# Value products of a two-layer attention issued behind a step's transposes in place of in front of them

## The chip, the cores and the metric

The kernel runs on one core of one Trainium2 chip. The metric is the device time of one execution in microseconds (us); less is better. All data are float32; most products are made of three matmuls over a high and a low part of each operand.

## The reference

The program computes two pairs of transformer layers, one after the other, on 512 tokens of width 1024 (batch 1). The first pair is a mixer with window attention, Fourier mixing and a short convolution, and is not touched here. The second pair (`hybrid_layer`, run for two layers) is, per layer and cut to what matters:

```
a_in, b_in, c_in = split(x @ w_in)
o_a = dilated_mixture(...)        # 6 heads of 64, bias and band as one mask
o_b = rms_norm(diff_attention(...)) # 4 heads: (softmax(q1 k1) - lam * softmax(q2 k2)) @ v
o_c = causal_attention(...)       # 6 heads, q and k of 96, v of 64
h = layer_norm(ALPHA * x + concat(o_a, o_b, o_c) @ w_o)
x = layer_norm(ALPHA * h + (silu(h @ w_gate) * (h @ w_up)) @ w_down)
```

All three attentions are causal, so a block of 128 queries number i (0 to 3) needs 128 (i + 1) keys.

## The kernel before

The program is written out engine by engine, with semaphores between them. The weights come as tiles of 128 x 2048 through three buffers; ScalarE writes each tile's high part, GpSimd its low part (L927). The change lies in the attention sweep of the second pair's layers.

**Units.** A unit is one head and one block of queries. A head of kind b has two maps, so each of its blocks gives two units, called first and second here; heads of kinds c and a give one. There are 80 units (`UNITS`, L705), and 64 of them are turned and multiplied with the values (`RANKS`): a first map is not, it is folded into its second. The first eight units are scored earlier, among the projections.

**Steps.** TensorE, VectorE and ScalarE go through the same steps, 5 to 83. For unit s, in step s:

- TensorE scores it (`score`, L2252 for kinds b and c, L2248 and L2249 for a) into one of three banks.
- VectorE adds the mask and takes the minimum (`scored`, L2986), out of PSUM into one of five buffers `sc`. The rows are negated, so that this is the maximum.
- ScalarE takes the exponential in place (`exp2`, L1563 for kind b, L1566 else).
- Two steps later, if the unit is a second map, VectorE joins the two maps (`pair`, L2994, L2995 and L2996): second times a ratio plus first. The result is what the transposes of a second map read.
- Four steps later TensorE turns it (L2367): i + 1 transposes of 128 x 128 into one of three other banks. They wait for `s_paired` (a second map) or `s_probs` (any other), and for the bank.
- ScalarE copies the turned rows to SBUF (L1602, into places called `raw`, `pt_rows`, `pt_cos` and `pt_vc` by the trace).

**Groups.** The turned units are gathered in 13 groups (`GROUPS`) of 4 to 6 units: four blocks of one head of kind c or a, and the b units that fall among them. `mix(g)` issues the products of a whole group with the values (L2346), 20 to 32 matmuls of 64 or 65 columns (two records of the trace each) into one of two banks; it waits for ScalarE's copy of every unit. It is issued in the step that turns the second unit behind the group's last. VectorE takes the rows of a group out (`rows_out2`, L3050 to L3062) one turned unit later. Group 12, the last, is issued among the first matmuls of the output projection (L2384).

The twelve steps and what they turn (kind, head and block of queries; a second map has a double prime):

```
group   0    1      2    3    4      5    6      7    8    9    10   11
turned  c0.3 b1.2"  c2.3 c3.0 b2.2"  c5.0 b3.0"  a1.3 a2.0 a3.0 a4.0 a5.2
```

Every few steps TensorE also turns a finished 128-column chunk of the attention's output (`turn_chunk`, L2325); ScalarE writes its high part (L1616), VectorE its low part (L2530). Its bank is one of the two of the groups.

Of the kernel before, what the change touches and what calls it, by code (L numbers as in the profile page):

```python
# [262 lines left out]
def _program(nc, I, out, seen):  # L263
    ctx = ExitStack()
    with ctx:
# [444 lines left out]
        def probs_of(i):  # L710

            return strips[:, B_HEADS + EARLY_AT[i], :] if i < EARLY else sc2[(i - EARLY) % N_B]
# [5 lines left out]
        def turns(step):  # L718
            i = step - (N_B - 1)
            return UNITS[i]["rank"] if 0 <= i < len(UNITS) else None  # L720
# [5 lines left out]
        GROUPS, MIXED, group_of = [[]], {}, {}  # L726
# [21 lines left out]
        def pt_place(y, r):  # L748

            u, landing = UNITS[RANKS[r]], raw_of((y, "up"))  # L750
            if u["kind"] == "b":
                where, a = ((pt_rows, 768), (landing, 1792), (pt_vc, 0), (landing, 1280))[u["i"]]
            elif group_of[r] % 2 == 0:
                where, a = landing, (1152, 896, 512, 0)[u["i"]]
            else:
                where, a = ((pt_rows, 640), (pt_rows, 384), (pt_rows, 0), (pt_cos, 0))[u["i"]]
            return where[:, a:a + u["n"]]
# [9 lines left out]
        def copied_by_vector(r):  # L767
            return False
# [84 lines left out]
        def _(sp):  # L853
            for half in range(2):
                t = 2 * half
                sp.dma_start(res[:, t:t + 2, :], I["x"][0, t * P:(t + 2) * P, :].rearrange("(t p) d -> p t d", p=P)).then_inc(s_x_landed[half].sem, 16)
            for n, (what, _) in enumerate(stream):
                if what == Q0:
                    sp.dma_start(raw_q0[:], I["tiles"][n, :, :]).then_inc(s_q0_landed.sem, 16)
# [834 lines left out]
        def _(pe):  # L1694
# [475 lines left out]
            for l in range(DEPTH):  # L2170
# [64 lines left out]
                def score(i):  # L2235

                    u, b = UNITS[i], S_BANKS[i % N_S]
                    pe.wait_ge(*emptied[b])
                    emptied[b] = s_scored.after((y, i))
                    if u["kind"] == "c":  # L2240
                        pe.wait_ge(s_roped.sem, s_roped.at((y, 1)))
                        pe.wait_ge(s_kr_all.sem, s_kr_all.at((y, u["head"])))
                        pe.wait_ge(s_proj.sem, s_proj.at((y, "qn", 2, 1)))
                    if u["kind"] == "a":
                        h = u["head"]
                        pe.wait_ge(s_a_lo.sem, s_a_lo.at((y, 2)))
                        pe.wait_ge(s_k_low.sem, s_k_low.at((y, h)))
                        pe.matmul(ps[:, b, 0:u["n"]], u["q"], u["k"], start=True, stop=False)  # L2248
                        pe.matmul(ps[:, b, 0:u["n"]], u["q"], K_LOW[h][:, 0:u["n"]], start=False,  # L2249
                                  stop=True).then_inc(s_scores.sem, s_scores.nth((y, i)))  # L2250
                    else:
                        pe.matmul(ps[:, b, 0:u["n"]], u["q"], u["k"], start=True, stop=True).then_inc(s_scores.sem, s_scores.nth((y, i)))  # L2252
# [63 lines left out]
                def turn_chunk(k, b):  # L2316

                    pe.wait_ge(*emptied[b])
                    emptied[b] = s_lo.after((y, "m", k))
                    if 3 <= k < 5:  # L2320
                        pe.wait_ge(s_sub.sem, s_sub.at(y))
                    else:
                        pe.wait_ge(s_o_out.sem, s_o_out.at((y, max(group_of[last_of[w]] for w in chunk_heads[k]))))
                    for t in range(XT):
                        m = pe.transpose(ps[:, b, P * t:P * t + P], ao[:, t, P * k:P * k + P], ident[:])  # L2325
                    m.then_inc(s_aot.sem, s_aot.nth((y, k)))

                def mix(g):

                    kinds = {UNITS[RANKS[r]]["kind"] for r in GROUPS[g]}  # L2330
                    pe.wait_ge(*emptied[OUT_BANKS[g % 2]])
                    emptied[OUT_BANKS[g % 2]] = s_o_out.after((y, g))
                    if "c" in kinds:
                        pe.wait_ge(s_proj.sem, s_proj.at((y, "vc", XT - 1)))
                        pe.wait_ge(s_vc_ones.sem, s_vc_ones.at(y))
                    if "a" in kinds:
                        pe.wait_ge(s_va_ones.sem, s_va_ones.at(y))
                    for r in GROUPS[g]:
                        u, (b, a), turned = UNITS[RANKS[r]], MIXED[r], pt_place(y, r)
                        if copied_by_vector(r):  # L2340
                            pe.wait_ge(s_pt_b.sem, s_pt_b.at((y, r)))
                        else:
                            pe.wait_ge(s_pt.sem, s_pt.at((y, r)))
                        for j, v in enumerate(u["vs"]):
                            for half in (0, HD):
                                m = pe.matmul(ps[half:half + HD, b, a:a + v.shape[1]], turned[:, P * j + half:P * j + half + HD], v,  # L2346
                                              start=j == 0, stop=j == len(u["vs"]) - 1)
                    m.then_inc(s_mixed.sem, s_mixed.nth((y, g)))
# [3 lines left out]
                for step in range(FROM, STEPS):  # L2352
                    if EARLY + N_S <= step < len(UNITS):
                        score(step)
                    r = turns(step)
                    if r is not None:
                        if r - 2 in (group[-1] for group in GROUPS):
                            mix(group_of[r - 2])
                        i, b = RANKS[r], TURNED["unit", r]
                        if UNITS[i]["second"]:  # L2360
                            pe.wait_ge(s_paired.sem, s_paired.at((y, i)))
                        else:
                            pe.wait_ge(s_probs.sem, s_probs.at((y, i)))
                        pe.wait_ge(*emptied[b])
                        emptied[b] = s_pt_b.after((y, r)) if copied_by_vector(r) else s_pt.after((y, r))
                        for j in range(len(UNITS[i]["vs"])):
                            m = pe.transpose(ps[:, b, P * j:P * j + P], probs_of(i)[:, P * j:P * j + P], ident[:])  # L2367
                        m.then_inc(s_turned.sem, s_turned.nth((y, r)))
                    if step in turn_at:
                        turn_chunk(turn_at[step], TURNED["chunk", turn_at[step]])  # L2370
                for kh in (0, 1):
# [955 lines left out]
```

## Time and profile before

| | us |
|---|---|
| median of 3 runs | 1829.53 (1829.01 to 1832.6) |
| the profiled execution | 1828.74 |
| its span, first to last instruction | 1826.9 |
| TensorE busy | 1779.0 (97%) |
| VectorE busy | 1196.8 (66%) |
| ScalarE busy | 912.8 (50%) |
| GpSimd busy | 777.8 (43%) |
| attention sweep, layer 0 of the second pair | 744 to 818 of the span |
| attention sweep, layer 1 | 1342 to 1416 of the span |

The profiled execution took 1.8 us more than its span. The engine shares are means over stages with different limits. The two sweeps repeat each other 597.9 us apart, to within 0.1 us.

### The profile page before, as it was taken

What the parts mean: (1) busy time and instruction counts of PE and PEld (TensorE: products, weight loads), DVE (VectorE), ACT (ScalarE), POOL (GpSimd) and SP (SyncE); (2) the same over time, 40 slices, a digit from 0 to 9 for tenths busy, and PEclk for the clock granted to TensorE, in tenths of its full rate; (3) what the DMA queues carried; (4) which work ended last, traced back from release to release, by engine and by line L of the source; (5) the groups of instructions that cost most, each with busy time, mean ns of one, the idle gap of its engine ahead of it and who ended that gap; (6) DMA issues with size and microseconds to landing.
All of it is one profiled execution on the core that took longest, in us unless ns stands there. A gap on an engine that the chain in (4) does not pass through costs nothing.

```text
span 1826.9 us, 33474 instructions
## 1 busy us (share of the span) xinstructions
PE 1779.0 (97%) x13078; PEld 1585.0 (87%) x13078; DVE 1196.8 (66%) x2313; ACT 912.8 (50%) x1789; POOL 777.8 (43%) x601
## 2 busy tenths in 40 slices
PE   9999999999999999989999999999998999999997
PEld 7898888878898888678999998888877899999886
DVE  5797465269455353785999984256368589998533
ACT  4242276484366474883545443227488255444323
POOL 2544262255553454344443436544424354343652
PEclk9999999999999999999999999999999999999999
DMA  8444141123221232103232323222310323323321
GB/s 337 168 173 167 24 116 60 69 70 139 104 48 55 88 102 107 42 2 139 93 111 98 116 93 126 100 88 92 117 42 2 138 72 114 116 93 116 116 93 46
DMA packets 37032, 182.40 MB, mean 100 GB/s; under 512 B 8288, under 2 KB 9184, under 8 KB 18956
## 3 DMA queue, kind: packets, MB, share of 16 engines
q1 hardware_dynamic: 30664, 168.89, 26.5%
q10 hardware_dynamic: 6212, 11.36, 2.0%
q8 instruction: 106, 1.74, 0.4%
q14 instruction: 50, 0.41, 0.1%
HBM read 178.10 MB, written 5.41 MB: 100 GB/s over the span
## 4 chain that ended last, share of the span: by engine, by line
PE 85%; DVE 8%; ACT 4%; issue 2%; POOL 1%; DMA 1%; DVEq 0%; SPq 0%; ACTq 0%
PE ps L1718 17%; PE ps L1720 17%; PE ps L1719 17%; PE ps L2441 7%; PE ps L2443 7%; PE ps L2442 7%; PE ps L1798 2%; PE ps L1812 2%; PE ps L2346 2%; PE ps L2252 2%; PE ps L1779 1%; PE ps L2367 1%; DVE sc L2986 1%; POOL w_lo L927 1%; ACT pt L1184 1%
## 5 line engine op out<-in xcount | busy, mean ns | idle before, releaser
L927 POOL TENSOR_TENSOR w_lo<-raw,w_hi 128x512 fp32r<-128x512 f32 (+1 forms) x343 | 477.9, 1426 | 616.1 <-ACT w_hi L1057 615.9
L1057 ACT ACTIVATE w_hi<-raw 128x1024 fp32r<-128x1024 f32 (+3 forms) x174 | 170.9, 1026 | 225.8 <-PE ps L1720 208.8
L1033 POOL TENSOR_TENSOR w_lo<-raw,w_hi 128x512 fp32r<-128x512 f32 x80 | 112.7, 1408 | 222.9 <-ACT w_hi L1122 222.7
L1718 PE MATMUL ps<-h_hi,w_lo 128*128 128x512 f32 (+1 forms) x496 | 177.2, 357 | 3.7 <-DVE h_lo L2530 3.6
L1719 PE MATMUL ps<-h_lo,w_hi 128*128 128x512 f32 (+1 forms) x496 | 174.5, 352 | 0.0
L1720 PE MATMUL ps<-h_hi,w_hi 128*128 128x512 f32 (+1 forms) x496 | 174.5, 352 | 0.0
L1718 PE MATMUL ps<-w_hi,hid_lo 128*128 128x512 f32 x352 | 137.1, 390 | 0.0
L1719 PE MATMUL ps<-w_lo,hid_hi 128*128 128x512 f32 x352 | 137.0, 389 | 0.0
L1720 PE MATMUL ps<-w_hi,hid_hi 128*128 128x512 f32 x352 | 136.9, 389 | 0.0
L2530 DVE TENSOR_TENSOR hid_lo<-hid,hid_hi 128x512 fp32r<-128x512 f32 x44 | 65.4, 1529 | 102.1 <-ACT hid_hi L1158 102.1
L1718 PE MATMUL ps<-w_hi,g_lo 128*128 128x512 f32 (+3 forms) x320 | 114.1, 356 | 1.5 <-POOL w_lo L927 1.5
L1720 PE MATMUL ps<-w_hi,g_hi 128*128 128x512 f32 (+3 forms) x320 | 112.1, 350 | 0.0
L1719 PE MATMUL ps<-w_lo,g_hi 128*128 128x512 f32 (+3 forms) x320 | 111.8, 349 | 0.0
L1718 PEld LDWEIGHTS ps<-h_hi,w_lo 128*128 128x128 f32 x496 | 93.8, 189 | 18.6 <-issue 5.5
L1720 PEld LDWEIGHTS ps<-h_hi,w_hi 128*128 128x128 f32 x496 | 93.7, 189 | 12.9
L1719 PEld LDWEIGHTS ps<-h_lo,w_hi 128*128 128x128 f32 x496 | 93.8, 189 | 11.7
L2592 DVE SCALAR_TENSOR_TENSOR acc<-raw,cond,acc 128x512 f32<-128x512 f32 x112 | 98.9, 953 | 0.8 <-DMA raw<-in_tiles 0.7
L1122 ACT ACTIVATE ext_hi<-ps 128x512 fp32r<-128x512 f32 x80 | 47.8, 598 | 95.1 <-DVE ps L3163 69.6
L2441 PE MATMUL ps<-T_hi,w_lo 128*128 128x256 f32 x320 | 90.7, 283 | 0.0
L2441 PE MATMUL ps<-G_hi,w_lo 128*128 128x256 f32 x320 | 90.6, 283 | 0.0
L2442 PE MATMUL ps<-G_lo,w_hi 128*128 128x256 f32 x320 | 90.6, 283 | 0.0
L2443 PE MATMUL ps<-G_hi,w_hi 128*128 128x256 f32 x320 | 90.6, 283 | 0.0
(392 smaller groups left out, 5446.0 us busy)
## 6 DMA issues: line engine op xcount, KB each, us to landing
raw<-in_tiles SPq DMA_DIRECT2D x139, 1024.0 KB, 4.8
strips<-bias_rows ACTq DMA_DIRECT2D x18, 256.0 KB, 4.0
raw<-in_tiles SPq DMA_DIRECT2D x4, 832.0 KB, 4.2
bias_rows<-bias_row SPq DMA_DIRECT2D x10, 320.0 KB, 9.9
raw<-in_tiles SPq DMA_DIRECT2D x4, 768.0 KB, 5.1
res<-in_x SPq DMA_DIRECT2D x2, 1024.0 KB, 6.4
ln<-in_ln_g ACTq DMA_DIRECT2D x4, 512.0 KB, 5.0
ln<-in_ln_b ACTq DMA_DIRECT2D x4, 512.0 KB, 7.6
```

The lines of the kernel that those rows point to most:

```text
L927: pool.tensor_tensor(w_lo[:, i % SPLIT, a:e], raw_of(what)[:, a:e], w_hi[:, i % SPLIT, a:e].bitcast(F32), ALU.subtract).then_inc(s_tile_lo ...
L1033: pool.tensor_tensor(lo, quad_of(what[0], j, name), hi.bitcast(F32), ALU.subtract).then_inc(s_pool_piece.sem, s_pool_piece.nth(((what[0], ...
L1057: act.activation(w_hi[:, i % SPLIT, a:b], raw_of(what)[:, a:b], ACT.Copy).then_inc(s_tile_hi.sem, s_tile_hi.nth((what, n)))
L1122: act.activation(piece_of(y, j, name)[0], src, ACT.Copy).then_inc(s_piece_hi.sem, s_piece_hi.nth((what, name)))
L1718: pe.matmul(o, lhs[1], rhs[0], start=first, stop=False)
L1719: pe.matmul(o, lhs[0], rhs[1], start=False, stop=False)
L1720: return pe.matmul(o, lhs[0], rhs[0], start=False, stop=last)
L2441: pe.matmul(o, lhs[1], rhs[0], start=starts and k == 0, stop=False, skip_group_check=True)
L2442: pe.matmul(o, lhs[0], rhs[1], start=False, stop=False, skip_group_check=True)
L2443: m = pe.matmul(o, lhs[0], rhs[0], start=False, stop=ends and k == 3, skip_group_check=True)
L2530: V.tensor_tensor(dst, src, hi.bitcast(F32), ALU.subtract).then_inc(s_lo.sem, s_lo.nth(key))
L2592: V.scalar_tensor_tensor(to[:], w, by, to[:], ALU.mult, ALU.add).then_inc(s_weigh.sem, s_weigh.nth((what, k, h)))
```

## The change

In each of the twelve steps in which a group's value products are issued, `mix` now stands behind the step's transposes. Before, TensorE's order in such a step is: score of unit s, value products of the group, transposes. Now it is: score, transposes, value products. A chunk's transposes, where a step has them, stay last.

```diff
                     r = turns(step)
                     if r is not None:
-                        if r - 2 in (group[-1] for group in GROUPS):
-                            mix(group_of[r - 2])
                         i, b = RANKS[r], TURNED["unit", r]
                         if UNITS[i]["second"]:
                             pe.wait_ge(s_paired.sem, s_paired.at((y, i)))
...
                         for j in range(len(UNITS[i]["vs"])):
                             m = pe.transpose(ps[:, b, P * j:P * j + P], probs_of(i)[:, P * j:P * j + P], ident[:])
                         m.then_inc(s_turned.sem, s_turned.nth((y, r)))
+                        if r - 2 in (group[-1] for group in GROUPS):
+                            mix(group_of[r - 2])
```

The orders of VectorE, ScalarE, GpSimd and SyncE are the same in both kernels. Two places of TensorE's order follow; a row of value products with x8 is eight matmuls. Line 2367 of the kernel before is 2365 of the changed one.

The first is group 1 in layer 0 of the second pair. Before:

```order
L2252 MATMUL ps<-bk,bq 128x256
L2346 MATMUL ps<-vb,raw 64x64 x8
L2346 MATMUL ps<-vc,pt_cos 64x65 x8
L2346 MATMUL ps<-vc,pt_rows 64x65 x2
L2346 MATMUL ps<-vb,pt_rows 64x64 x2
L2346 MATMUL ps<-vc,pt_rows 64x65 x10
L2367 MATMUL ps<-ident,sc_0_145 128x128 x3
L2252 MATMUL ps<-bk,bq 128x256
```

And now:

```order
L2252 MATMUL ps<-bk,bq 128x256
L2365 MATMUL ps<-ident,sc_0_145 128x128 x3
L2346 MATMUL ps<-vb,raw 64x64 x8
L2346 MATMUL ps<-vc,pt_cos 64x65 x8
L2346 MATMUL ps<-vc,pt_rows 64x65 x2
L2346 MATMUL ps<-vb,pt_rows 64x64 x2
L2346 MATMUL ps<-vc,pt_rows 64x65 x10
L2252 MATMUL ps<-bk,bq 128x256
```

The three transposes of a second map (`sc_0`, block 2 of head 1 of kind b) have come from behind the 30 products to the place ahead of them.

The second is group 11, at the sweep's end, with the first matmuls of the output projection (L1718 to L1720) and the last group. Before:

```order
L2325 MATMUL ps<-ident,ao 128x128 x4
L2346 MATMUL ps<-va,pt_cos 64x65 x8
L2346 MATMUL ps<-va,pt_rows 64x65 x12
L2367 MATMUL ps<-ident,sc_4_149 128x128 x3
L2367 MATMUL ps<-ident,sc_0_145 128x128 x2
L2367 MATMUL ps<-ident,sc_1_146 128x128
L1718 MATMUL ps<-w_hi,g_lo 128x512
L1719 MATMUL ps<-w_lo,g_hi 128x512
L1720 MATMUL ps<-w_hi,g_hi 128x512
L2346 MATMUL ps<-va,raw 64x65 x20
```

And now:

```order
L2325 MATMUL ps<-ident,ao 128x128 x4
L2365 MATMUL ps<-ident,sc_4_149 128x128 x3
L2346 MATMUL ps<-va,pt_cos 64x65 x8
L2346 MATMUL ps<-va,pt_rows 64x65 x12
L2365 MATMUL ps<-ident,sc_0_145 128x128 x2
L2365 MATMUL ps<-ident,sc_1_146 128x128
L1718 MATMUL ps<-w_hi,g_lo 128x512
L1719 MATMUL ps<-w_lo,g_hi 128x512
L1720 MATMUL ps<-w_hi,g_hi 128x512
L2346 MATMUL ps<-va,raw 64x65 x20
```

The three transposes of `sc_4` have come ahead of group 11; the last three transposes, the projection's first matmuls and the last group stand as they did.

## Rows read from the trace of the kernel before

**Rows 1.** The page's first part: busy us, share of the span, instructions.

```profile
PE   1779.0 (97%) x13078; PEld 1585.0 (87%) x13078; DVE 1196.8 (66%) x2313; ACT 912.8 (50%) x1789; POOL 777.8 (43%) x601
```

**Rows 2.** Windows: stretch, its length, busy us by engine, granted clock, DMA share, GB/s.

```profile
744.00:818.00 74.00, 65.56 (x851) 52.79 (x851) 59.72 (x234) 61.53 (x162) 31.24 (x34) 1.00 0.08 23
1342.00:1416.00 74.00, 65.52 (x852) 52.89 (x851) 59.60 (x234) 61.51 (x162) 31.12 (x34) 1.00 0.08 24
```

**Rows 3.** Waits of PE, 744 to 820: total us, times, longest us.

```profile
PE ps L2367 <- DVE sc L2996: 6.8, 8, 1.5
PE ps L2252 <- DVE small L2986: 0.8, 1, 0.8
PE ps L2248 <- DVE small L2986: 0.4, 1, 0.4
```

**Rows 4.** Timeline, group 1: start us, us, engine, line, out<-in, [idle before <-releaser].

```profile
756.63 0.69 PE L2346 MATMUL ps<-vb,raw 128*64 128x64 f32 x16
...
757.29 0.62 DVE L2996 SCALAR_TENSOR_TENSOR sc<-sc,small,sc 128x384 f32<-128x384 f32 x1
...
758.53 0.55 PE L2367 MATMUL ps<-ident,sc 128*128 128x128 f32 x3
...
758.83 0.36 PE L2252 MATMUL ps<-bk,bq 128*128 128x256 f32 x1
```

**Rows 5.** Timeline, group 4.

```profile
778.24 0.80 PE L2346 MATMUL ps<-vc,raw 128*64 128x65 f32 x20
...
778.93 0.62 DVE L2996 SCALAR_TENSOR_TENSOR sc<-sc,small,sc 128x384 f32<-128x384 f32 x1
...
779.67 0.55 PE L2367 MATMUL ps<-ident,sc 128*128 128x128 f32 x3
```

**Rows 6.** Timeline, group 6, and the next wait behind it.

```profile
792.84 0.80 PE L2346 MATMUL ps<-vc,raw 128*64 128x65 f32 x20
792.87 1.28 POOL L944 CAST free_hi<-ka 64x512 fp32r<-64x512 f32 x2 [2.23 <-PE ps L2249]
...
793.22 0.41 DVE L2996 SCALAR_TENSOR_TENSOR sc<-sc,small,sc 128x128 f32<-128x128 f32 x1
...
794.74 0.18 DVE L3056 RECIPROCAL recips<-ps 128x4 f32<-128x4 f32 x1 [0.22 <-PE ps L2346]
...
798.01 0.55 PE L2367 MATMUL ps<-ident,sc 128*128 128x128 f32 x3 [0.66 <-DVE sc L2996]
```

**Rows 7.** Timeline, behind groups 1 and 4.

```profile
760.34 0.69 DVE L2986 CUSTOM_DVE_ANT_0 sc<-ps,strips_g 128x512 f32<-128x512 f32 x1 [0.33 <-PE ps L2252]
...
762.22 0.44 PE L2367 MATMUL ps<-ident,sc 128*128 128x128 f32 x2 [0.40 <-DVE sc L2996]
...
783.77 0.44 PE L2367 MATMUL ps<-ident,sc 128*128 128x128 f32 x2 [0.91 <-DVE sc L2996]
```

**Rows 8.** Timeline, a `pair` of 128 columns elsewhere.

```profile
772.84 1.22 DVE L2996 SCALAR_TENSOR_TENSOR sc<-sc,small,sc 128x128 f32<-128x128 f32 x1
```

**Rows 9.** Timeline, behind groups 0 and 8.

```profile
751.36 0.60 ACT L1602 ACTIVATE raw<-ps 128x512 f32<-128x512 f32 x1 [1.75 <-PE ps L2346]
...
807.96 0.18 DVE L3056 RECIPROCAL recips<-ps 128x4 f32<-128x4 f32 x1 [1.34 <-PE ps L2346]
```

**Rows 10.** Timeline, group 11 to the last group.

```profile
818.48 0.69 PE L2346 MATMUL ps<-va,pt_cos 128*64 128x65 f32 x16
...
819.92 0.18 DVE L3056 RECIPROCAL recips<-ps 128x4 f32<-128x4 f32 x1 [2.00 <-PE ps L2346]
...
820.38 0.49 ACT L1602 ACTIVATE raw<-ps 128x384 f32<-128x384 f32 x1 [0.91 <-PE ps L2367]
820.77 0.59 ACT L1616 ACTIVATE g_hi<-ps 128x512 fp32r<-128x512 f32 x1
...
821.46 0.69 DVE L2530 TENSOR_TENSOR g_lo<-ps,g_hi 128x512 fp32r<-128x512 f32 x1 [0.91 <-ACT g_hi L1616]
...
822.21 0.57 PE L2346 MATMUL ps<-va,raw 128*64 128x65 f32 x12 [0.84 <-DVE g_lo L2530]
```

**Rows 11.** Waits of ACT, 744 to 820: total us, times, longest us.

```profile
ACT raw L1602 <- PE ps L2367: 1.6, 3, 0.7
```

## The prediction

> **What bounds the kernel now.** The page's first part [rows 1] shows TensorE busy for 97% of the span, so the program as a whole is TensorE's, and a microsecond that TensorE loses or saves should show in the end, unless another engine paces that place. The windows view of the second pair's two attention sweeps [rows 2] shows that this place is different: of 74 us TensorE is busy for 65.6 and 65.5, VectorE for 59.7 and 59.6, ScalarE for 61.5 and 61.5, so three engines run closely coupled and TensorE is idle for 8.4 us per sweep. The two rows agree within 0.1 us; what I read in the first sweep (layer 0) counts twice. The waits view [rows 3] says what ends TensorE's idle time: eight times a probability row that VectorE has just written (L2996, `pair`), 6.8 us together, and twice VectorE's scored row, 1.2 us. So TensorE stands still mostly in front of the transposes (L2367) of a second map, whose data `pair` delivers last. Each value group of 1.3 to 1.9 us that stands ahead of such transposes hides a part of that wait. The question for each of the twelve moved groups is therefore: when is the input of the transposes ready, compared with the start of the group?
>
> **The change, part by part.** No instruction is added or removed. VectorE's, ScalarE's, GpSimd's and the DMA queues' orders stay as they are; only TensorE's moves, at twelve places per layer (groups 0 to 11; group 12 is issued elsewhere). In the rows nothing of TensorE overtakes a transpose that waits, so what is held behind a blocked transpose is now the whole group, the next scores and everything VectorE and ScalarE take from them.
>
> *Three groups whose transposes need `pair`.* At groups 1, 4 and 6 the step turns a second map. Group 1 [rows 4]: products start at 756.63, `pair` writes until 757.29 + 0.62 = 757.91, the transposes run at 758.53. The wait was hidden. Now the transposes are issued first. In the rows a released transpose starts about 0.06 behind the writer's end, so they start at 757.97, 1.34 us after the point at which the products used to start; the group then follows in full, and the next scores (758.83) come 1.34 later. Group 4 [rows 5]: 778.93 + 0.62 + 0.06 = 779.61 against 778.24, 1.37 us. Group 6 [rows 6]: 793.22 + 0.41 + 0.06 = 793.69 against 792.84, 0.85 us; here VectorE itself waited for the group (794.74, 0.22 idle) and so gets it later by 0.85 plus one transpose, 0.13: 0.98, and the next wait of TensorE (798.01) hangs on VectorE. Sum 1.34 + 1.37 + 0.98 = 3.69 us per layer.
>
> Is the loss swallowed by the waits that TensorE has further on (0.40 at 762.22, 0.91 at 783.77, 0.66 at 798.01; [rows 6, 7])? I take it that it is not. Between group 1 and the wait at 762.22 VectorE sat idle for 0.33 until TensorE's scores (760.34, [rows 7]): the chain to that `pair` runs through a score issued behind the group, so the delay goes through VectorE and comes back whole. The same order of events stands before 783.77.
>
> The 0.41 of group 6's `pair` is read while GpSimd runs a cast (792.87, [rows 6]). Another `pair` of the same 128 columns took 1.22 us (772.84, [rows 8]). I use 0.41, since neither the cast nor this `pair` moves. The Trainium skill, GPSIMD Engine Reference, section Key points, says that GpSimd shares its SBUF interfaces with VectorE and that instructions with two SBUF inputs, as `pair` is, contend. By that rule 1.22 would be the size to expect, 0.81 more per layer, and the forecast 1.6 us later (1837.7); the row speaks against it here.
>
> *The nine other groups.* Their transposes read what ScalarE finished steps earlier, so nothing is waited for: transposes and products only change places, and the next scores start when they did. What moves is the end of the products, later by one to four transposes (three take 758.83 − 758.53 = 0.30, [rows 4]), and the end of the transposes, earlier. Who waits for the products? Group 0: a ScalarE copy (751.36, 1.75 idle, [rows 9]) into a place that group 0 still reads, now later by up to 0.4. ScalarE is not what TensorE waits for next; bounds 0 and 0.4, I take 0.1. Group 8: VectorE (807.96, 1.34 idle, [rows 9]), later by one transpose, 0.1. For the rest the bounds are 0 and 0.30 each, and I take 0, since VectorE comes to their rows later than the products end or, at group 2, waits for a score right behind them.
>
> *Group 11 gains.* [Rows 10]: the last chunk's high part (ScalarE, 820.77) is queued behind the copy at 820.38, which waits for transposes issued behind group 11. VectorE's low part (821.46) waits for it, and the last group on TensorE (822.21) for that low part, 0.84 us. With the transposes in front, the copy and the high part are early; VectorE's rows of group 11 (819.92) come 0.3 later and take 0.6, so the low part starts near 820.85 in place of 821.46. I count −0.6 per layer; bounds 0 and −0.84.
>
> **Sum**: 3.69 + 0.1 + 0.1 − 0.6 = 3.3 per layer, +6.6 us. On the profiled execution's 1828.74 that is 1835.3. The median of the three runs lies 0.8 higher (1829.53), so the forecast for the median is **1836.1**. Not seen in the trace: the gaps where TensorE passes from transposes to products and from products to scores; I bound them by 0.1 either way per place, 24 places, 2.4 us. A measurement of this kernel can tell about 0.2% (3.7 us) from no change; 6.6 is beyond it.
>
> **The rivals.**
> - *Later waits absorb the loss.* If VectorE set the pace, 0.40, 0.91 and 0.66 would come off: 0.94 + 0.46 + 0.32 + 0.2 − 0.6 = 1.3 per layer, 1832.1, within 0.2%. For it: VectorE is busy for 81% of the sweep. Against it: its idle 0.33 until TensorE's scores. 0.15.
> - *Faster: the earlier transposes pay.* ScalarE sat idle for 1.6 us per sweep for such transposes [rows 11]. If ScalarE and VectorE pace the sweep, the three new waits fall inside the 8.0 us that TensorE waits anyway, and ScalarE's 1.6 comes back beside group 11's 0.6: −4.4, 1825.1. It decides if the waits at the later transposes shrink by as much as the new ones add. Against it: ScalarE's end is never the last thing TensorE waits for in [rows 3]. 0.09.
> - *Every group costs.* The products' end is later by 0.30 at all nine others and VectorE hands it on: 5.4 more, 1841.5. 0.10.
> - *The clock.* The granted clock is 1.00 in both sweeps [rows 2], with a wait of 1.5 us in them [rows 3]. If it fell to 1.2 GHz behind each of the six new waits for one group and its transposes (1.90 + 0.30, [rows 4]), 13.2 us more, 1849.3. The Trainium skill, TensorE: Matmul & The Clock Gate, Part 1 and Part 4, says that an idle TensorE is throttled and that transposes do not count as busy in the same way. The transposes and the long wait now in the sweeps took nothing off the clock. 0.02.
> - That the change does nothing is excluded: the order shows the groups moved.
>
> **How the numbers follow.** The forecast's own case has 0.64, from 1833 to 1839 (group 11 at its bounds, the gaps, the collision); 0.04 of it lies within 0.2%. Slower: 0.60 + 0.10 + 0.02 = 0.72. Same: 0.15 + 0.04 = 0.19. Faster: 0.09. The range leaves out the faster case, the clock, the upper half of "every group costs" (0.06) and the foot of "absorb" (0.03), 0.2 in all: 1831.0 to 1840.5.
>
> **What would show it.** Right: the waits of transposes for `pair` rise from 8 to 11 per sweep and from 6.8 to about 10.4 us; the waits after them (0.40, 0.91, 0.66) keep their size; each sweep grows by some 3.3 us; TensorE's wait before the last group shrinks from 0.84 to about 0.2; granted clock 1.00. Wrong: the later waits shrink by the amount of the new ones, or the sweeps are as long as before.

## The result, and the profile after

The changed kernel takes 1839.32 us (median of 4 runs, 1837.06 to 1840.67), the kernel before, run beside it, 1830.26 (4 runs, 1829.01 to 1832.6). The ratio is 1.0045, 95% interval 1.0034 to 1.0057: slower by about 9 us, where 1836.1 was forecast and 1831.0 to 1840.5 was the range.

| | before | after |
| - | - | - |
| span of the profiled execution, us | 1826.9 | 1836.8 |
| first sweep, first waiting transposes to last group, us | 73.58 | 77.32 |
| second sweep, the same, us | 73.57 | 77.33 |
| start of the first sweep, us | 748.63 | 751.07 |

The sweeps are measured between two events that every kernel of this study has: the start of the sweep's first transposes that wait for VectorE (a wait of 1.32 us that is the same everywhere) and the start of the last group on TensorE, which before is the 822.21 row in [rows 10]. They account for 3.74 + 3.76 = 7.5 us. From the last group of the second sweep to the end of the span it is 406.82 us before and 406.81 after. The other 2.44 us lie ahead of the first sweep, where the two programs are the same. That start fell between 748.63 and 752.10 in the twelve profiles of this study, and the profile of before has the earliest of them; chunk_copy_first, for one, has before's order on TensorE and starts at 751.18. So the 2.4 us can't be put down to the change, and sweep lengths are the finer measure below. They repeated within 0.11 us from one layer to the other in every kernel.

The page's first part, after; it stands against [rows 1]:

```profile
PE 1781.7 (97%) x13078; PEld 1586.3 (86%) x13078; DVE 1197.6 (65%) x2313; ACT 911.4 (50%) x1789; POOL 777.4 (42%) x601
```

The counts are the same, and the engines' busy times moved by under 3 us. Windows of the two sweeps (columns as in [rows 2], but of 77.4 and 77.3 us):

```profile
751.00:828.40 77.40, 66.91 (x887) 54.00 (x887) 57.52 (x228) 60.32 (x160) 28.03 (x28) 1.00 0.08 22
1352.70:1430.00 77.30, 66.86 (x886) 53.94 (x886) 57.43 (x227) 60.20 (x160) 28.04 (x28) 1.00 0.08 23
```

TensorE's idle time in a sweep is now 77.40 − 66.91 = 10.5 us, where [rows 2] gave 8.4 of 74 us. The granted clock is 1.00 in both, so the clock has no part in this execution's sweeps; other executions are taken up under "The clock". Who ends TensorE's idle time, 744 to 826, as in [rows 3]:

```profile
PE ps L2365 <- DVE sc L2996: 10.2, 11, 1.6
PE ps L2252 <- DVE small L2986: 0.8, 1, 0.8
PE ps L2248 <- DVE small L2986: 0.4, 1, 0.4
```

Eleven waits for a joined map in place of eight, 10.2 us in place of 6.8. The timeline shows the three new ones: groups 1, 4 and 6, with the map's last write on VectorE, the transposes and the products behind them.

```profile
759.77 0.62 DVE L2996 SCALAR_TENSOR_TENSOR sc<-sc,small,sc 128x384 f32<-128x384 f32 x1
760.45 0.55 PE L2365 MATMUL ps<-ident,sc 128*128 128x128 f32 x3 [1.26 <-DVE sc L2996]
760.92 0.55 PEld L2346 LDWEIGHTS ps<-vb,raw 128*64 128x64 f32 x16 [0.17 <-issue]
...
762.82 0.39 PE L2252 MATMUL ps<-bk,bq 128*128 128x256 f32 x1
762.94 0.18 DVE L3056 RECIPROCAL recips<-ps 128x4 f32<-128x4 f32 x1 [1.73 <-PE ps L2346]
...
783.71 0.55 PE L2365 MATMUL ps<-ident,sc 128*128 128x128 f32 x3 [1.29 <-DVE sc L2996]
784.18 0.66 PEld L2346 LDWEIGHTS ps<-vc,raw 128*64 128x64 f32 x20 [0.17 <-issue]
...
798.87 0.40 DVE L2996 SCALAR_TENSOR_TENSOR sc<-sc,small,sc 128x128 f32<-128x128 f32 x1
799.33 0.33 PE L2365 MATMUL ps<-ident,sc 128*128 128x128 f32 x1 [0.77 <-DVE sc L2996]
799.59 0.66 PEld L2346 LDWEIGHTS ps<-vc,raw 128*64 128x64 f32 x20
...
801.49 0.18 DVE L3056 RECIPROCAL recips<-ps 128x4 f32<-128x4 f32 x1 [1.32 <-PE ps L2346]
```

In the first of them the map is written until 759.77 + 0.62 = 760.39, the transposes start 0.06 later, and 1.9 us of products that could have run in that wait come behind it. VectorE then stands idle for 1.73 us for these very products. The same timeline, at the waits that were to absorb the loss or to keep their size:

```profile
789.43 0.44 PE L2365 MATMUL ps<-ident,sc 128*128 128x128 f32 x2 [0.92 <-DVE sc L2996]
...
804.75 0.55 PE L2365 MATMUL ps<-ident,sc 128*128 128x128 f32 x3 [0.72 <-DVE sc L2996]
```

0.91 became 0.92 and 0.66 became 0.72 (the rows of before are in [rows 6, 7]); the 0.40 behind group 1 is still 0.40, now at 766.22. Nothing was absorbed. Last, the sweep's end, against [rows 10]:

```profile
825.66 0.69 PE L2346 MATMUL ps<-va,pt_cos 128*64 128x65 f32 x16
...
826.63 0.63 ACT L1616 ACTIVATE g_hi<-ps 128x512 fp32r<-128x512 f32 x1
...
827.10 0.18 DVE L3056 RECIPROCAL recips<-ps 128x4 f32<-128x4 f32 x1 [2.33 <-PE ps L2346]
...
827.65 0.68 DVE L2530 TENSOR_TENSOR g_lo<-ps,g_hi 128x512 fp32r<-128x512 f32 x1
...
828.39 1.33 PE L2346 MATMUL ps<-va,raw 128*64 128x65 f32 x38 [0.17 <-DVE g_lo L2530]
```

The last chunk's high part starts 0.97 behind group 11's first product (before: 820.77 − 818.48 = 2.29), VectorE's low part no longer waits for it, and the last group waits for 0.17 in place of 0.84.

### The profile page after: what moved, and what is told of

The parts are those of the page before. It is cut to its first block, busy times and chain, and to the rows that moved or that the text cites. A ratio compares the mean times of both kernels' runs of the same rounds, so it can differ in the third digit from the quotient of the medians.

```text
span 1836.8 us, 33474 instructions
## 1 busy us (share of the span) xinstructions
PE 1781.7 (97%) x13078; PEld 1586.3 (86%) x13078; DVE 1197.6 (65%) x2313; ACT 911.4 (50%) x1789; POOL 777.4 (42%) x601
## 4 chain that ended last, share of the span: by engine, by line
PE 84%; DVE 7%; ACT 4%; issue 2%; POOL 1%; DMA 1%; SPq 0%; DVEq 0%; ACTq 0%
PE ps L1718 17%; PE ps L1720 17%; PE ps L1719 17%; PE ps L2441 7%; PE ps L2443 7%; PE ps L2442 7%; PE ps L1798 2%; PE ps L2346 2%; PE ps L1812 2%; PE ps L1779 1%; PE ps L2365 1%; PE ps L2252 1%; DVE sc L2986 1%; DMA raw_q<-in_tiles 1%; POOL w_lo L927 1%
## 5 line engine op out<-in xcount | busy, mean ns | idle before, releaser
L1718 PE MATMUL ps<-h_hi,w_lo 128*128 128x512 f32 (+1 forms) x496 | 177.2, 357 | 4.6 <-DVE h_lo L2530 3.6
L1720 PE MATMUL ps<-h_hi,w_hi 128*128 128x512 f32 (+1 forms) x496 | 174.5, 352 | 0.0
L1718 PE MATMUL ps<-w_hi,hid_lo 128*128 128x512 f32 x352 | 137.1, 390 | 0.0
L1720 PE MATMUL ps<-w_hi,hid_hi 128*128 128x512 f32 x352 | 136.9, 389 | 0.0
L1718 PE MATMUL ps<-w_hi,g_lo 128*128 128x512 f32 (+3 forms) x320 | 114.0, 356 | 1.5 <-POOL w_lo L927 1.3
L1720 PE MATMUL ps<-w_hi,g_hi 128*128 128x512 f32 (+3 forms) x320 | 112.0, 350 | 0.0
L1718 PEld LDWEIGHTS ps<-h_hi,w_lo 128*128 128x128 f32 x496 | 93.8, 189 | 19.6 <-issue 5.5
L1720 PEld LDWEIGHTS ps<-h_hi,w_hi 128*128 128x128 f32 x496 | 93.7, 189 | 12.9
```

Source lines behind the costliest of these rows:

```text
L1718: pe.matmul(o, lhs[1], rhs[0], start=first, stop=False)
L1720: return pe.matmul(o, lhs[0], rhs[0], start=False, stop=last)
```

## The experiments

Ten kernels. The theory: only three of the twelve moves cost (groups 1, 4 and 6, whose transposes need a map that VectorE has not joined yet), one gains (group 11), and the other eight are worth next to nothing. The rivals: every group costs a little; the loss comes from the products' place, and not from the wait for the join. A "join" is the write of `pair`: VectorE's last write (L2996) of a second map.

### Three groups, nine groups, one group

Three kernels split the change. In each, `mix` is behind the transposes for a part of the groups only:

```diff
-                        if r - 2 in (group[-1] for group in GROUPS):
+                        ends = r - 2 in (group[-1] for group in GROUPS)
+                        behind = ends and group_of[r - 2] in (1, 4, 6)
+                        if ends and not behind:
                             mix(group_of[r - 2])
...
                         m.then_inc(s_turned.sem, s_turned.nth((y, r)))
+                        if behind:
+                            mix(group_of[r - 2])
```

only_second_maps has (1, 4, 6) there, all_but_second_maps (0, 2, 3, 5, 7, 8, 9, 10, 11), only_group_11 (11,).

> Products behind the transposes at groups 1, 4 and 6 alone, where a second map is turned; the nine other groups as before. My theory (the loss is TensorE's wait for the joined maps): each sweep 4.1 to 4.2 us longer, 8.3 us in all, slightly more than the full change, because group 11's gain is missing; the last group still waits 0.84 us for the low part. Rival (every moved group costs by the later end of its products): well under half of the change's 7.5 us in the two sweeps, since only 3 of 12 groups move.

> Products behind the transposes at groups 0, 2, 3, 5, 7, 8, 9, 10 and 11; groups 1, 4 and 6 as before. My theory: each sweep about 0.4 us shorter (0.2 to 0.3 lost at groups 0 to 10, 0.67 gained behind group 11), so 0.9 us in all, not to be told from no change by the times; 8 waits for the joined maps of 6.8 us per sweep, as before. Rival (every group costs): 3 to 5 us longer. Rival (the earlier transposes pay, ScalarE and VectorE pace the sweep): over 3 us shorter.

> Products behind the transposes at group 11 alone. My theory: the last group's wait for the low part falls from 0.84 to about 0.17 us in both sweeps, nothing else moves: 1.3 us less in all. Rival (the gain in the full change came from a TensorE that was late anyway): no shift of the last group against before.

| kernel | sweeps, us | to before (73.58/73.57) | median, us (before 1829.79) | ratio, 95% |
| - | - | - | - | - |
| only_second_maps | 77.75 / 77.72 | +4.16 | 1840.06 | 1.0056 (1.0042 to 1.0069) |
| all_but_second_maps | 73.16 / 73.15 | −0.42 | 1829.21 | 0.9997 (0.9988 to 1.0006) |
| only_group_11 | 72.88 / 72.89 | −0.69 | 1829.48 | 0.9997 (0.9988 to 1.0006) |

The waits of TensorE in the sweep, first of only_second_maps, where the transposes are L2369 and the joining write is L3000:

```profile
PE ps L2369 <- DVE sc L3000: 10.2, 11, 1.5
PE ps L2346 <- DVE g_lo L2534: 0.8, 1, 0.8
```

and of all_but_second_maps:

```profile
PE ps L2369 <- DVE sc L3000: 6.8, 8, 1.6
...
PE ps L2346 <- DVE g_lo L2534: 0.2, 1, 0.2
```

The three groups alone bring the three waits and keep the 0.8 before the last group. The nine others bring none and take that wait down. The parts add: 4.16 − 0.42 = 3.74, what the whole change costs per sweep. Group 11 gains 0.69, so the eight others cost 0.27 together, 0.03 each. "Every group costs" is refuted; the gain of group 11 is too small for a measurement of the whole kernel, though the sweeps show it in both layers.

### The same places without the wait for the join

The changed kernel, but at the three places the transposes read the second map before it is joined. The joined rows are written over the first map, so VectorE works as much as before; what this kernel leaves out is three joined blocks per layer, so its result is not the program's:

```diff
-                        if UNITS[i]["second"]:
+                        if UNITS[i]["second"] and i not in (18, 38, 52):
                             pe.wait_ge(s_paired.sem, s_paired.at((y, i)))
...
-                    V.scalar_tensor_tensor(probs_of(i)[:, 0:n], probs_of(i)[:, 0:n], ratio, probs_of(i - 1)[:, 0:n],
+                    V.scalar_tensor_tensor(probs_of(i - 1 if i in (18, 38, 52) else i)[:, 0:n], probs_of(i)[:, 0:n], ratio, probs_of(i - 1)[:, 0:n],
```

> The changed kernel, in which the transposes of groups 1, 4 and 6 read the second map as ScalarE leaves it; VectorE still computes the joined rows but writes them over the first map, so that its load is the same and three joined blocks per layer are missing from the result. My theory: with no wait for the join left at the three places, the sweep (77.32 us in the changed kernel, 73.57 before) falls to 73.2 to 73.9. Rival (the loss is the later end of the products, handed on by VectorE): it stays above 76.

Measured: sweeps of 74.04 and 74.06; median 1831.01 (before 1829.83), ratio 1.0006 (0.9997 to 1.0016). Its waits in the sweep:

```profile
PE ps L2365 <- DVE sc L2996: 6.9, 8, 1.6
```

Eight again. Of the 3.74 that the change costs, 77.32 − 74.04 = 3.28 went with the wait for the join, while the products stayed behind the transposes. The rival that blames the place of the products alone (above 76) is refuted. It can have a part in what is left: the sweeps missed the expected band (73.2 to 73.9) by 0.14 and lie 0.88 above those of all_but_second_maps. Its timeline at group 1 shows where some of it is:

```profile
758.73 0.31 PEld L2365 LDWEIGHTS ps<-ident,sc 128*128 128x128 f32 x3 [0.41 <-ACT sc L1563]
758.74 0.55 PE L2365 MATMUL ps<-ident,sc 128*128 128x128 f32 x3
759.21 0.42 PEld L2346 LDWEIGHTS ps<-vb,raw 128*64 128x64 f32 x11 [0.17 <-issue]
```

Here the transposes come so soon that ScalarE's exponential of that map is the last thing missing (the weight loads wait 0.41 for it); and the products start 0.47 behind the first transpose, with an idle gap of 0.17 in the weight loads that no engine ends.

### The join made later

If the join is what TensorE waits for, then a delay of the join must come back in full after the change, and mostly be hidden before it. At the three units the reciprocal ahead of the join is done three times (each about 0.19 us on VectorE, two of them added), in the kernel before and in the changed one:

```diff
-                    step(V.reciprocal(ratio, small[:, 1, i % 8:i % 8 + 1]))
+                    for _ in range(3 if i in (18, 38, 52) else 1):
+                        step(V.reciprocal(ratio, small[:, 1, i % 8:i % 8 + 1]))
```

> The kernel before, with the reciprocal ahead of the join repeated twice (about 0.19 us each, 0.38 together) at the three second maps that groups 1, 4 and 6 cover. My theory of cover: the joins end 0.62 ahead of the transposes at group 1, 0.12 at group 4 and 1.00 at group 6, so only group 4 shows the delay, by 0.3, and group 6 passes on some 0.2 through VectorE's rows: the sweep goes from 73.57 to 73.9 to 74.2. Rival (VectorE paces the sweep): 1.1 us longer, 74.7.

> The changed kernel with the same two repeated reciprocals at the same three maps. My theory: nothing covers the joins any more, so the 0.38 us shows in full at each of them: the sweep goes from 77.32 to 78.4 or 78.5. Rival (TensorE's waits are taken up later): under 0.5 us longer, at most 77.8.

Measured: in the kernel before, sweeps of 74.20 and 74.30 (+0.62, +0.73), median 1831.73, ratio 1.0010 (1.0001 to 1.0019). The first sweep lies at the upper end of the expected band (73.9 to 74.2), the second 0.1 above it, both under the rival's 74.7. At group 1 the delay is hidden; at group 4 the group's cover is just used up, and behind group 6 the delay travels on through VectorE, where the wait of 0.66 in [rows 6] became 0.91. Group 4's transposes:

```profile
780.55 0.55 PE L2367 MATMUL ps<-ident,sc 128*128 128x128 f32 x3 [0.25 <-DVE sc L2997]
```

In the changed kernel, sweeps of 78.79 and 78.90 (+1.47, +1.57 on the changed kernel's), ratio to before 1.0084 (1.0068 to 1.0101). The three waits went from 1.26, 1.29 and 0.77 to 1.66, 1.68 and 1.44. So the same delay costs more than twice as much once nothing stands between score and transposes. The sweeps came out 0.3 to 0.4 above the expected 78.4 to 78.5, and the third wait is the reason: it grew by 0.67, not by 0.4. The timeline of join_delayed_after there (the join is L2997):

```profile
797.50 1.28 POOL L944 CAST free_hi<-ka 64x512 fp32r<-64x512 f32 x2 [2.22 <-PE ps L2249]
...
798.25 0.68 DVE L2997 SCALAR_TENSOR_TENSOR sc<-sc,small,sc 128x128 f32<-128x128 f32 x1
798.86 2.63 POOL L947 TENSOR_TENSOR free_lo<-ka,free_hi 64x512 fp32r<-64x512 f32 x2
798.98 0.33 PE L2365 MATMUL ps<-ident,sc 128*128 128x128 f32 x1 [1.44 <-DVE sc L2997]
```

The row of L944 is two casts, the second from 798.17 to 798.78. The join starts 0.08 into this second cast and ends 0.14 behind its end; in the changed kernel it starts 0.35 into the first cast (798.52 to 799.13) and ends 0.15 behind that one's end. So its end moved by the distance of the two casts, 0.67, and not by the 0.39 that the reciprocals add. That a join which starts beside an instruction of GpSimd ends a fixed time behind that instruction is worked out from all profiles below.

The median of this kernel, 1845.97 of 4 runs (1839.77 to 1848.75), lies 6.2 us above its profiled execution. The sweeps explain 10.5 us over before, which is what the profiled execution shows (+11.0 on that of before). The other three runs took 1844.76, 1847.19 and 1848.75, and their mean granted clock is 0.996, 0.994 and 0.994, where the profiled execution has 0.998. A mean lower by 0.002 is 3.7 us of 1846 and one lower by 0.004 is 7.4 us (estimates from these numbers); measured are 5.0, 7.4 and 9.0 more. So most of it goes with a lower clock. In which stretch, and why, no profile shows.

### The chunk's high part, without moving any product

Group 11's gain came from a ScalarE queue: the last chunk's high part (L1616) stood behind a copy that waits for late transposes. That can be had alone. In the kernel before, ScalarE writes a turned chunk's high part at the beginning of its step:

```diff
                 for step in range(FROM, STEPS):
+                    if step - 1 in turn_at:
+                        k = turn_at[step - 1]
+                        act.wait_ge(s_aot.sem, s_aot.at((y, k)))
+                        act.activation(g_hi[:, CHUNKS.index(k), :], ps[:, TURNED["chunk", k], :], ACT.Copy).then_inc(s_hi.sem, s_hi.nth((y, "m", k)))
                     r = turns(step)
...
-                    if step - 1 in turn_at:
-                        k = turn_at[step - 1]
-                        act.wait_ge(s_aot.sem, s_aot.at((y, k)))
-                        act.activation(g_hi[:, CHUNKS.index(k), :], ps[:, TURNED["chunk", k], :], ACT.Copy).then_inc(s_hi.sem, s_hi.nth((y, "m", k)))
```

> TensorE's order as before; ScalarE writes the high part of a turned chunk at the beginning of its step, ahead of the copy of the turned unit and of the exponential. If the last group's wait is ScalarE's queue order, as my theory has it, the low part comes with VectorE's rows of group 11 and the wait of 0.84 us falls below 0.1 us. The chain of waits further says that VectorE idles 0.68 and 0.89 us for such a high part ahead of the waits at 789.56 (0.69) and 804.03 (1.51): these should shrink by 0.7 and 0.9. In all 1.7 to 4.8 us less than before. Rival (VectorE's idle time there costs nothing, or the delayed copies and exponentials take it back): 0 to 1.7 us less.

Measured: sweeps of 72.13 and 72.12 (−1.45), the shortest of all; median 1827.95 of 11 (1826.62 to 1832.34), before 1829.79; ratio 0.9992 (0.9983 to 1.0001). TensorE's matmuls show no wait before the last group any more (its weight loads still wait 0.37 for the low part, before 1.27), and VectorE's low part waits for no high part:

```profile
822.48 0.68 DVE L2530 TENSOR_TENSOR g_lo<-ps,g_hi 128x512 fp32r<-128x512 f32 x1
823.31 0.78 PEld L2346 LDWEIGHTS ps<-va,raw 128*64 128x64 f32 x24 [0.37 <-DVE g_lo L2530]
823.31 0.86 PE L2346 MATMUL ps<-va,raw 128*64 128x65 f32 x22
```

More than that came: in mid-sweep two waits (0.69 for a join, 0.39 for a scored row, 1.08 together) gave way to one:

```profile
793.56 0.44 PE L2248 MATMUL ps<-free_hi,qa 128*128 128x384 f32 x1 [0.58 <-DVE small L2986]
```

In before VectorE stood idle for 0.68 at 785.97 for the high part of the chunk turned in step 45; here it doesn't, so the join behind it starts earlier, by 0.56 counted from the sweep's start. It ends earlier by more than that, because it now starts beside GpSimd's cast and not beside its subtraction. In before:

```profile
787.68 2.96 POOL L947 TENSOR_TENSOR free_lo<-ka,free_hi 64x512 fp32r<-64x512 f32 x2
787.90 1.61 DVE L2996 SCALAR_TENSOR_TENSOR sc<-sc,small,sc 128x512 f32<-128x512 f32 x1
```

And in chunk_copy_first:

```profile
788.88 1.27 POOL L944 CAST free_hi<-ka 64x512 fp32r<-64x512 f32 x2 [1.47 <-PE ps L2252]
...
789.89 0.81 DVE L2996 SCALAR_TENSOR_TENSOR sc<-sc,small,sc 128x512 f32<-128x512 f32 x1
```

0.84 + 0.50 = 1.34 of the 1.45. The wait of 1.51 further on, which was expected to shrink by 0.9, did not (1.62): the join that it waits for ends 0.28 behind the end of a subtraction of GpSimd before and here.

### Which chunks

Is it the chunk of the mid-sweep place and the last that matter? Chunks are turned at steps 31, 45, 59, 72 and 80; "the middle one" is here the second, of step 45, whose low part starts at 785.97 in before. two_chunks_first meant to move the middle and the last high part alone, but named step 44 for the middle one, so it moved only the last (the first hunk has the same condition the other way round):

```diff
-                    if step - 1 in turn_at:
+                    if step - 1 in turn_at and step - 1 not in (44, 80):
```

> TensorE's order as before; ScalarE writes the high part first in its step only for the chunks turned in steps 44 and 80, not for those of steps 31, 55 and 71. With all five first the sweep was 72.13 us and the wait at 804.03 grew from 1.51 to 1.62. My theory: the gain is that of steps 44 and 80 alone (0.5 and 0.87), and the 0.1 lost goes away: 72.0 to 72.15 us per sweep, 3 us less than before in all. Rival (the other three chunks gave part of it): 72.3 to 72.9.

Measured: sweeps of 72.66 and 72.67 (−0.92), median 1828.10, ratio 0.9991 (0.9982 to 1.0000). As a test of two chunks it failed by its step number (72.66 lies in the rival's band, which here says nothing for that rival); as one of the last chunk alone it says that the last is worth 0.92. The mended kernel has 45 in place of 44:

> As two_chunks_first, with the right step: the middle chunk is turned in step 45, not 44, so that run moved only the last one (sweep 72.66, 0.92 shorter than before). Moved here: the chunks of steps 45 and 80. My theory: the high part of step 45 stands in the chain to the wait at 789.56, so this gives the 0.5 us more that all five gave, without the 0.1 lost at 804: 72.0 to 72.15 per sweep, 3 us less than before in all. Rival (the 0.5 came from the other chunks): 72.5 to 72.7.

Measured: sweeps of 72.22 and 72.21 (−1.36), median 1828.73 beside 1831.4 for before, ratio 0.9986 (0.9978 to 0.9995). The middle chunk is worth 0.44, and with the last it gives 1.36 of the 1.45 that all five give. It missed the upper end of its band by 0.07, far from the rival's 72.5 to 72.7. It is the one version whose interval lies below 1; its median gain, 2.67 us, stands beside 1.36 × 2 = 2.7 from the sweeps.

Last, the other half of the queue: only the last chunk's high part first, and VectorE's low parts one step later, so that VectorE would not wait for a high part at all.

```diff
-                    if st - 2 in turn_at:
-                        k = turn_at[st - 2]
+                    if st - 3 in turn_at:
+                        k = turn_at[st - 3]
```

> The last chunk's high part first, as before; the others stay, and VectorE writes each chunk's low part one step later, so that it does not stand idle for ScalarE's high part (1.10, 0.68 and 0.89 us in the kernel before). My theory: the idle 0.68 and 0.89 stand in the chains to the waits at 789.56 and 804.03, so the sweep falls from 72.66 to 71.5 to 72.0. Rival (VectorE then waits for scores or products instead): 72.4 to 72.7.

Measured: sweeps of 72.49 and 72.47, median 1828.95, ratio 0.9991 (0.9982 to 1.0000). The gain expected did not come; its rival's 72.4 to 72.7 held. The middle place was cured as with the two chunks (the 0.69 and 0.39 became 0.58), but a later low part made TensorE wait for it at another chunk:

```profile
816.21 1.39 PE L2350 MATMUL ps<-va,raw 128*64 128x65 f32 x40 [0.33 <-DVE g_lo L2534]
```

## Why the prediction was right, and which term was mis-sized

**What bounds the sweeps**: right. The waits for joined maps set the loss; they rose from 8 to 11 and from 6.8 to 10.2 us, where "about 10.4" was forecast.

**Groups 1, 4 and 6**: the mechanism was right, and three experiments bear it out (the three moves alone, the join unawaited, the join delayed). The join's end and the 0.06 behind it came out exactly: with the 2.48 us by which the first place lay later than before, the transposes' 760.45 is 757.97, the forecast start. The size was off. Forecast 1.34, 1.37 and 0.98, sum 3.69; measured from before's events to after's, less the shift that each place already had, 1.52, 1.55 and 1.08, sum 4.15, and the kernel with these three moves alone gave 4.16. The term of the sum that was mis-sized is the sentence that the group follows and "the next scores (758.83) come 1.34 later", together with gaps bounded at 0.1 per place. After three transposes the products start 0.47 behind the first (760.45 to 760.92); a score after three transposes started 0.30 behind (758.53 to 758.83 in [rows 4]). The 0.17 between is the gap that the weight loads show. At group 6, behind a single transpose, the products start 0.26 behind it (799.33 to 799.59), where 0.13 was counted. In before, the weight loads stood idle ahead of group 1's products too (0.24), but that was over before the 756.63 from which I counted; now it comes behind the wait. This also fits the eight groups that don't wait: for them the gap only changes its place, and they cost 0.03 each on average. That reading of the gap is from the rows; no run took the gap away alone.

**Are the losses absorbed?** No, as forecast: 0.40, 0.91 and 0.66 became 0.40, 0.92 and 0.72. join_delayed_before shows the other side: a delay that a group of products covers is hidden, and one that is not travels through VectorE to the next wait.

**The size of group 6's join.** It took 0.40, as the 0.41 of [rows 6] had said, but the prediction read that row wrongly: a cast does not leave the join alone. A join of 128 columns with GpSimd idle is shorter still; in before:

```profile
753.30 0.35 DVE L2996 SCALAR_TENSOR_TENSOR sc<-sc,small,sc 128x128 f32<-128x128 f32 x1
```

And the 1.22 of [rows 8] ran from 772.84 beside these instructions of GpSimd (a row x2 is two instructions):

```profile
771.29 1.28 POOL L944 CAST free_hi<-ka 64x512 fp32r<-64x512 f32 x2 [3.47 <-PE ps L2252]
772.65 2.61 POOL L947 TENSOR_TENSOR free_lo<-ka,free_hi 64x512 fp32r<-64x512 f32 x2
```

The first L947 ended at 773.91 and the join at 774.06, 0.15 later. The first cast of [rows 6] ended at 793.48 and group 6's join at 793.63, again 0.15 later. The twelve profiles hold 288 joins, and each of them ends, to within 0.01 us, at the later of two times: its start plus its time alone, or the end of the cast or subtraction that GpSimd was running when it started, plus a fixed rest. 117 of them were held in this way (none of the 72 of 384 columns, which never started beside GpSimd).

| columns | alone, us | rest behind GpSimd's end, us |
| - | - | - |
| 128 | 0.35 | 0.15 |
| 256 | 0.49 | 0.28 |
| 512 | 0.75 | 0.55 |

So a join's length depends on how far into GpSimd's instruction it starts, and not on which instruction that is. Group 6's join starts 0.35 into a cast in both kernels. The ground that neither of them moves was sound, and 0.41 the right size; that "the row speaks against" contention was not. The Trainium skill, GPSIMD Engine Reference, section Key points, has VectorE's instructions with two SBUF inputs contend with GpSimd; the traces here agree, for the cast and for the subtraction alike. The forecast with 1.22 in that place, 1837.7, would have lain nearer to the measured time, but by a slowdown that did not happen.

**Group 11**: −0.6 forecast, −0.67 in the changed kernel and −0.69 alone. **Groups 0 and 8**: 0.1 each forecast; the eight groups together cost 0.27, against 0.2. Group 0's copy waited for 2.2 us in place of 1.75, and group 0 shifted the sweep by 0.04.

**The clock**: 1.00 in both sweeps of the profiled execution, as forecast. The Trainium skill, TensorE: Matmul & The Clock Gate, Part 1, has an idle TensorE throttled; waits of up to 1.68 us (join_delayed_after), with transposes behind them, took nothing off the granted clock of the profiled sweeps. The executions without a profile are less clear. The three kernels with the three new waits (changed kernel, only_second_maps, join_delayed_after) have a mean granted clock of 0.997 or less in 8 of their 13 executions; all other kernels together have it in 12 of 161. In the changed kernel the two at 0.998 took 1837.06 and 1838.63, the two at 0.997 1840.01 and 1840.67. Whether the new waits sometimes bring the clock down, as the clock's rival had it on a much larger scale, is not shown: the profiled executions are all at 0.998 or 0.999.

**The sum**: 3.3 per layer was forecast, 3.75 came. Twice 0.45 is 0.9 us; of the rest of the 3.2 us between the forecast and the median 1839.32, 0.7 is that before's own median came out at 1830.26 in place of 1829.53. The last 1.6 or so are not placed. Two things of that size are on record: the start of the first sweep moved by up to 3.5 us between profiles, and a mean granted clock lower by 0.001, as in two of the four runs, is 1.8 us of 1838 (an estimate). No run separates them. So the forecast time lay 3.2 us low, of which the sweeps' share is 0.9.

## What to carry to other kernels

Independent work that an in-order queue issues ahead of a blocking wait is cover, and moving it behind the wait costs what it covered, and here 0.1 to 0.2 us more per place; where nothing is awaited the move is nearly free, so ask of each place when the awaited operand is ready. If one of twelve moves gains, look for the queue that it unblocked: here it was ScalarE's, and putting one short copy ahead there, without touching TensorE, gained more (0.92 per sweep for the last chunk alone) than the move had (0.69). And when one instruction of VectorE takes 0.4 us here and 1.6 there, look at what GpSimd runs at its start.

## What the runs showed of the hardware that was not expected

- VectorE's join, which reads two tensors in SBUF, ended 0.15, 0.28 or 0.55 us (128, 256 or 512 columns) behind the end of the GpSimd instruction beside which it started, cast or subtraction alike, in all 117 cases of twelve profiles in which that instruction held it up. A delay of 0.39 us (three reciprocals took 0.55, one 0.16) therefore moved such a join by 0.67, the distance of two casts. In before, three of the eight waits for a join (0.91, 0.69 and 1.51 us) stand behind joins that took 0.79, 1.61 and 1.10 us where 0.49, 0.75 and 0.49 is their time alone: 1.8 us per sweep in which VectorE is held. What of this would come back if GpSimd's instructions stood elsewhere, no run shows.
- Between three or four transposes and 64-column value products TensorE's weight loads stand idle for 0.17 us, with no engine that ends the wait, at groups 0, 1, 2, 4, 7 and 11 of the changed kernel alike; behind a single transpose it was 0.12 at groups 6, 8 and 9.
- The same delay of 0.4 us at three places cost 0.62 to 0.73 us per sweep with products ahead of the transposes and 1.47 to 1.57 with products behind them.
